# The order in which the SBUF tiles of a two-block transformer kernel are declared

## The reference

```python
# first block
xn = rmsnorm(h, norm_mix_g)
q_a, k_a, v_a, q_b, f_b, i_b, og_b, g_a, g_b = split_cols(xn @ w_in)          # 1024 x 9216
y_a = moba_attention(q_a, k_a, v_a, positions) @ w_br_attn
y_b = hgrn2(q_b, f_b, i_b, og_b, lb, hgrn_norm_g) @ w_br_hgrn
h = h + (sigmoid(g_a) * y_a + sigmoid(g_b) * y_b) @ w_out
h = h + memory_cross_attention(rmsnorm(h, norm_x_g), rmsnorm(mem, norm_mem_g), wq_x, wkv_x, wo_x)
gu = rmsnorm(h, norm_ffn_g) @ w_ffn_in
h = rmsnorm(h + (silu(gu[..., :2816]) * gu[..., 2816:]) @ w_ffn_out, final_norm_g)
# second block, for layer in (0, 1)
x = x + 0.5 * swiglu(rmsnorm(x, ffn1_norm), ffn1_w_in, ffn1_w_out)
x = x + mixer(rmsnorm(x, mix_norm))                   # NSA, then differential attention
x = x + 0.5 * swiglu(rmsnorm(x, ffn2_norm), ffn2_w_in, ffn2_w_out)
```

## The kernel before, in words

| tile | bytes | starts at | of 128 | of 256 |
|---|---|---|---|---|
| RAW, WH, WL | 24,576 each | 16,512; 41,088; 65,664 | 0 | 128 |
| R0 (scale per token) | 1,056 | 90,240 | 0 | 128 |
| XR, HT | 16,384; 8,192 | 91,296; 107,680 | 32 | 160 |
| PAR (gains) | 604 | 115,872 | 32 | 160 |
| CON (constants) | 5,136 | 116,480 | 0 | 0 |
| MSK, SB, PT, TMP, STAT | 512 to 6,144 | 121,632 on | 32 | 32 or 160 |
| FA, with XM on it | 32,768 | 142,112 | 32 | 32 |
| FB, with XF, XS, XO on it | 53,248 | 174,880 | 32 | 32 |

## Time and profile before

### The profile page before, as it was taken

The page is one execution under the profiler, slowest core; times in us unless marked ns, Lnnn a source line. Parts: engine busy times, 40 slices in busy tenths (PEclk is TensorE's granted clock), DMA queues, the critical chain, the costliest instruction groups (busy, mean ns, idle before and its releaser), DMA issues.

```text
span 1661.4 us, 27287 instructions
## 1 busy us (share of the span) xinstructions
PE 1628.8 (98%) x11554; PEld 1468.6 (88%) x11554; DVE 1222.6 (74%) x1482; ACT 929.9 (56%) x1249; POOL 153.3 (9%) x63
## 2 busy tenths in 40 slices
PE   8999999999999999999999899999999999999999
PEld 7999989999988888888897688888888888788888
DVE  6888868664688768986578768866887657678864
ACT  7966778455544455444487854444544547764442
POOL 0000000000022101220000002210222000002210
PEclk9999999999999999999999799999999999999999
DMA  7554433544355465545543235546554563345544
GB/s 279 179 178 159 148 140 140 184 172 177 128 203 185 147 208 198 203 170 174 204 156 123 83 125 196 186 156 201 211 193 162 176 223 132 123 148 184 193 157 131
DMA packets 44618, 283.82 MB, mean 171 GB/s; under 512 B 4944, under 2 KB 6608, under 8 KB 17744
## 3 DMA queue, kind: packets, MB, share of 16 engines
q1 hardware_dynamic: 44352, 281.99, 48.2%
q10 hardware_dynamic: 144, 0.08, 0.0%
HBM read 281.00 MB, written 1.05 MB: 170 GB/s over the span
## 4 chain that ended last, share of the span: by engine, by line
PE 83%; DVE 7%; ACT 6%; issue 2%; DMA 1%; SPq 0%; DVEq 0%; ACTq 0%
PE bank L516 82%; ACT WH L1227 3%; DVE WL L1816 2%; ACT SB L1352 1%; DVE STAT L1974 1%; DMA RAW<-in_w_in 1%; PE bank L698 1%; ACT XM L1234 0%; DVE XM L1824 0%; DVE HT L1872 0%; DVE SB L1971 0%; DVE FB L1842 0%; ACT FB L1251 0%; ACT XR L1234 0%; DVE FA L2271 0%
## 5 line engine op out<-in xcount | busy, mean ns | idle before, releaser
L1816 DVE TENSOR_TENSOR WL<-RAW,WH 128x2048 fp32r<-128x2048 f32 (+1 forms) x282 | 590.2, 2095 | 163.9 <-ACT WH L1227 159.4
L1227 ACT ACTIVATE WH<-RAW 128x2048 fp32r<-128x2048 f32 (+1 forms) x282 | 494.0, 1755 | 356.2 <-PE bank L516 351.8
L516 PE MATMUL bank<-XR,WH 128*128 128x256 f32 (+1 forms) x2608 | 644.9, 326 | 3.4 <-DVE WL L1816 2.5
L516 PE MATMUL bank<-XR,WL 128*128 128x256 f32 x1832 | 514.3, 281 | 0.0
L516 PEld LDWEIGHTS bank<-XR,WH 128*128 128x128 f32 x2608 | 435.0, 188 | 50.3 <-issue 3.6
L516 PEld LDWEIGHTS bank<-XR,WL 128*128 128x128 f32 x1832 | 345.4, 189 | 0.1
L516 PE MATMUL bank<-XF,WH 128*128 128x512 f32 x880 | 305.3, 392 | 0.0
L516 PE MATMUL bank<-XM,WH 128*128 128x512 f32 (+1 forms) x960 | 290.9, 363 | 3.5 <-DVE XM L1824 1.9
L516 PE MATMUL bank<-XF,WL 128*128 128x256 f32 x880 | 246.0, 280 | 0.0
L516 PE MATMUL bank<-XM,WL 128*128 128x256 f32 x832 | 232.6, 280 | 0.0
L516 PEld LDWEIGHTS bank<-XM,WH 128*128 128x128 f32 x960 | 171.2, 188 | 34.4 <-DVE XM L1824 3.5
(11 more groups left out here) (288 smaller groups left out, 1730.3 us busy)
## 6 DMA issues: line engine op xcount, KB each, us to landing
RAW<-in_f1i SPq DMA_DIRECT2D x44, 1024.0 KB, 4.8
RAW<-in_f2i SPq DMA_DIRECT2D x44, 1024.0 KB, 4.8
RAW<-in_w_in SPq DMA_DIRECT2D x35, 1024.0 KB, 4.8
RAW<-in_w_ffn_in SPq DMA_DIRECT2D x22, 1024.0 KB, 4.8
RAW<-in_f1o SPq DMA_DIRECT2D x32, 704.0 KB, 4.1
RAW<-in_f2o SPq DMA_DIRECT2D x32, 704.0 KB, 4.2
RAW<-in_diff_w_in SPq DMA_DIRECT2D x12, 1024.0 KB, 4.9
RAW<-in_w_ffn_out SPq DMA_DIRECT2D x16, 704.0 KB, 4.2
```

Of the source, the lines that this page charges most:

```text
L516: return e.matmul(o, l, r, start=start, stop=stop)
L1227: e.activation(split_at(u, cols)[0], RAW[:, u % NRAW, 0:cols], ACT.Copy).then_inc(hi_done.tick(u), 1)
L1816: e.tensor_tensor(lo, RAW[:, u % NRAW, 0:cols], hi.bitcast(f32), sub).then_inc(lo_done.tick(u), 1)
```

## The change

Of the fifteen declarations eight small tiles move behind FB, in another order. No size, no instruction, no wait and no transfer is edited.

```diff
         RAW = sb("RAW", [128, NRAW, 2048])
         WH = sb("WH", [128, NW, 2048], f32r)
         WL = sb("WL", [128, NW, 2048], f32r)
-        R0 = sb("R0", [128, 264])
         XR = sb("XR", [128, 2, 2048], f32r)
         HT = sb("HT", [128, 8, S])
-        PAR = sb("PAR", [128, NPAR])
-        CON = sb("CON", [128, NCON])
-        MSK = sb("MSK", [128, 8, 64], u8)
-        SB = sb("SB", [128, 4, 384])
-        PT = sb("PT", [128, 3, 384])
-        TMP = sb("TMP", [128, 3, 512])
-        STAT = sb("STAT", [128, 768])
         NA, NB = 4, 5
...
         FB = sb("FB", [128, NB * 2048 + 1024 + 2048])
+        CON = sb("CON", [128, NCON])
+        SB = sb("SB", [128, 4, 384])
+        PT = sb("PT", [128, 3, 384])
+        TMP = sb("TMP", [128, 3, 512])
+        STAT = sb("STAT", [128, 768])
+        MSK = sb("MSK", [128, 8, 64], u8)
+        R0 = sb("R0", [128, 264])
+        PAR = sb("PAR", [128, NPAR])
```

## The result

| | before | after |
|---|---|---|
| median (range) | 1660.3 us (1659.32 to 1662.68, 4 runs) | 1677.31 us (1668.59 to 1682.54, 4 runs) |
| span of the profiled execution | 1661.4 us | 1666.8 us |

The ratio is 1.0092 with the interval [1.0056, 1.0127]: slower by some 0.9%, and with a spread of 14 us where the kernel before has 3. The forecast was 1660 us, no change, and the range up to 1666. Execution and span after: 1668.59 and 1666.8 us, so a span is 1.8 us shorter than the execution's time. The prediction set the span of before, 1661.4, beside execution times; by this it was an execution of some 1663.2 us, slower than all four in the table.

What follows compares the result with a forecast made beforehand. TensorE (PE) was taken to bound the kernel; DVE, ACT, POOL 0, transfers 0 to -0.1 us and PE 0 left the profiled 1661.4 us unchanged, a median of 1660 us; own range 1657 to 1663, with slower rival and small gain 1655.5 to 1666.

Steps and rivals of the forecast that it cites:

- PE is the path: Whole kernel: TensorE bounds it, busy 1628.8 of 1661.4 us, with 82% of the chain in the matmul helper.
- DVE, ACT and POOL don't feel them: Weight splitting and POOL's product: new places cost 0; bounds 2 us for splits, 1.3 us on POOL.
- weights still land in 4.8 us: Weight transfers into RAW, which doesn't move: one megabyte lands in 4.8 us, effect taken as 0.
- the clock: Clock rival: the half-level dip at 921 to 935 us goes or recurs, 7 us either way (1652.5 or 1666.5); chance 5%.
- line 1816 at 2.29 us and line 1227 at 1.91: Weight splitting on DVE and ACT: these times staying unchanged was a sign that the forecast is right.
- I take 0: PE's 2640 pairs and 1512 triples: no change in time expected from the new starts.
- the pair doesn't feel that much of its place: Feed-forward pairs: three take 1.04 us with x in XR and in XF, so 0 change was taken.
- the bound of 3 ns: Pairs: 0.01 us over three leaves 3 ns per pair either way, 8 us over 2640 pairs.
- pairs off 0.347 by more than 1 ns: Pairs on PE: the sign of being wrong altogether, since 1 ns over 2640 pairs is 2.6 us.
- the one case of before in which both operands have the same remainder of 128, as all will have after: Triples with both operands from x tiles (XO,XR): 356 ns each, used as the example for after.
- The slower rival: PE's triples, above all from XR: equal remainders slow them from 350 to 355 or 356 ns, 4 to 6 us, 1664.5 us; 20%.
- The one on transfers: x's landing in HT: by the skill's 256-byte rule, one 32-byte beat in some 133 saved, 0.04 us.

Runs made afterwards that it cites:

- the matmuls alone: One weight unit and x tiles at set distances from the weights, PE only, no network: triples 340 to 360 ns, pairs 347 to 353 at multiples of 32 bytes.
- the second trace of the changed kernel: The changed kernel run again with no edit: 1675.77 us, ratio 1.009 against the kernel before; span of the profiled execution 1673.8 us.
- the run with 128 bytes: Changed kernel plus 128 unused bytes between WL and XR, so x begins 128 bytes past the weights' remainder of 256: 1679.07 us, ratio 1.0109 against the kernel before.
- the run with 32 bytes: Changed kernel plus 32 unused bytes between WL and XR, so x tiles begin 32 bytes past the weights' remainder: 1662.22 us, ratio 1.0007 against the kernel before.

## Why the prediction was wrong

**Read rightly.** PE is the path; the edit acts by nothing but places; DVE, ACT and POOL don't feel them (2284, 1900 and 2692 ns for operands that moved); weights still land in 4.8 us; the clock moved the time by some microseconds. The sign that it gave for the first two, line 1816 at 2.29 us and line 1227 at 1.91, could not have failed: RAW, WH and WL stay where they were.

**The step that failed is PE's.** "I take 0" for pairs and triples both. For the pairs the rows compared XR with XF, at distances 32 and 160, found them equal, and concluded that "the pair doesn't feel that much of its place". The table of the matmuls alone shows what that equality was: two of the three good columns. Neither row had the condition that was coming, distance 0, and the bound of 3 ns from the digit of two agreeing rows was no bound for a third place; 353 against 347 is twice that, and comes and goes, 3.4 us for each of five feed-forwards. Even the 8 us that it worked out from those 3 ns was left out of the range, which ends at 1666. Its own sign of being wrong altogether, "pairs off 0.347 by more than 1 ns", came true in the second trace of the changed kernel.

**The triples.** The prediction took XO,XR for "the one case of before in which both operands have the same remainder of 128, as all will have after". They were 128 bytes apart of 256, which stood in the table of starts, and after the change all are 0 apart. 356 was the price of 128 (and came back as 356 in the run with 128 bytes), 360 that of 0: 10.7 us over the 1512 triples, where the prediction had 0. In the run with 32 bytes, XO and XR have the same place of 256, and their triples took 360 while all others took 350 to 355.

**The rival that happened.** The slower rival had the place and the sign, with 20%, and it had the cause in part: the relation of the two operands, but as equal remainders of 128, while 96 bytes apart costs as much (1.0104). Its price of 4 to 6 us held 5 to 6 ns for a triple from XR where it was 9, and left the pairs at nothing. With 10.7 us for the triples and up to 17 for the feed-forwards it would have given 1660 + 10.7 = 1671 with all feed-forwards at the fast cadence and 1688 with all at the slow one, give or take the few microseconds of the clock; the eight runs of the changed kernel lie from 1668.59 to 1682.54. The trace had also said that one tile has two cadences (XS at 350 and at 355): where there are several states, the equality of two samples is a weak ground for a third.

**The rules weighed.** The one on transfers stays untested at its 0.04 us: the rule as the prediction cites it speaks of bytes that are fetched, while HT is written, and the landing of x in HT took 5.0 us in the trace after and 4.7 to 5.2 in the other traces, a scatter beyond the 0.1 us that the prediction allowed. One that bears on the step that failed: the Trainium skill, "SBUF — State Buffer", section "A bandwidth-pool intuition that's wrong (but worth ruling out)", gives TensorE a second, independent read port for weight loads. Read as saying that moving reads and weight loads don't disturb each other whatever their places, it would have supported the forecast. The measurement doesn't fit that reading: 340 to 360 ns for the same three matmuls by nothing but the distance of the two operands. That the weight load ahead of a matmul meets the moving read of the one at work is a possible cause, and no run shows it; nor is it known why several cadences exist or what chooses among them.

## What to carry to other kernels

In a kernel that PE bounds, the distance between the starts of moving and stationary operand, modulo 256 bytes, can be worth 1% (1.0092 to 1.0109 at distances 0, 96 and 128 here, 1.0007 at 32), and rounding tiles to "nice" starts can land on one of the bad values; measure it with a loop of the real matmuls, and then in the network. Any edit of SBUF declarations ahead of matmul operands moves that distance, so a change elsewhere can be charged with or credited for it; pin the starts when comparing. Two rows that agree bound a quantity only between the conditions that they had.

## What the runs showed of the hardware

- A triple of 256-column float32r matmuls takes 340 to 360 ns and a 512 + 256 pair 347 to 360 ns at the granted clock 1.00, by the distance of the operands modulo 256 bytes (the matmuls alone). Moving both operands by 32 bytes left the loss as it was (1679.93 us).
- A whole feed-forward of some 183 us (528 pairs) keeps its cadence, 347 or 353 ns a pair at distance 0, and takes either from execution to execution (358.37 and 178.19 us in one trace of the changed kernel, 358.38 and 181.58 in the other). With the clock's half-level stretches it makes part of a spread of 14 us where the kernel before has 3; how much of it, no trace of the slowest executions tells.
- Steps of 16 bytes still change the numbers (340 at 16, 350 to 353 at 32 for triples with x moving).
